# Two moves in the projections of a four-block transformer kernel: rotations split over two chunks, and modulation vectors turned one weight unit later

## The chip, the cores and the metric

The kernel runs on one core of one Trainium2 chip. The metric is the device time of one execution in microseconds, the median over several runs. One profiled execution, taken by the hardware profiler, gives the trace that the rows below come from. In names of the profile PE is TensorE (PEld its weight loads), DVE is VectorE, ACT is ScalarE, POOL is GpSimd, SP is SyncE, which issues the transfers from memory.

## The reference

512 tokens of width 1024 pass through two hybrid layers (`first_block`), then, joined by 256 context tokens, through an even and an odd layer, each with a feed-forward part (`second_block`). All is in float32. What the change touches is the start of a layer: a modulation computed from the conditioning vector, a normed and modulated input, one large in-projection, and rotary embeddings on some of its columns.

```python
def hybrid_layer(x, c_act, positions, w_mod, b_mod, pre_gain, post_gain, w_in, ...):
    mod = c_act @ w_mod + b_mod
    shift, scale, gate = jnp.split(mod[:, None, :], 3, axis=-1)
    h = rms_norm(x, pre_gain) * (1.0 + scale) + shift
    proj = h @ w_in                      # 3088 columns
    (aq, ak, av, ag, rq, rk, rv, rg, gq, gk, gv, gg, ga) = jnp.split(proj, IN_SPLITS, axis=-1)
    aq = apply_rotary(aq.reshape(B, S, ATTN_HEADS, HEAD_DIM), positions, rope_freq)
    ak = apply_rotary(ak.reshape(B, S, ATTN_KV_HEADS, HEAD_DIM), positions, rope_freq)
    a_out = sliding_window_attention(aq, ak, av, sinks) * jax.nn.silu(ag)
    rq = apply_rotary(rq.reshape(B, S, RET_HEADS, RET_DK), positions, ret_freq)
    rk = apply_rotary(rk.reshape(B, S, RET_HEADS, RET_DK), positions, ret_freq)
    ...
    y = jnp.concatenate([a_out, r_out, g_out], axis=-1) @ w_out
    return x + gate * rms_norm(y, post_gain)
```

The even and odd layers of the second block have the same frame with other mixers, and their modulation has two conditions, one for tokens and one for context.

## The kernel before, in words

The program is a list of phases; each engine walks through the list and does its own part of each phase. Most phases end in a barrier of four engines (phase_end); Linear with a residual, the norms and a few others flow into the next.

**Linear** (from line 676) is a projection. Its output columns are cut into chunks, for the sliding layers (layers 0 and 1, `layer_one`, line 1739) five of 512 columns, one of 272 and one of 256; they are counted from 0 here. The rows are token tiles of 128: four in the sliding layers, six (with the context) in the even ones. The 1024 input features of a chunk are read in four weight units (q = 0 to 3) of 256 features.

For each unit SyncE loads the raw weights into one of four slots of `w_raw` (weights_load), ScalarE rounds them to the high half `w_hi` (weights_high, line 288), GpSimd subtracts to get the low half `w_lo` (weights_low, line 295), and TensorE waits for that (weights_use) and does three matmuls for every tile and 128 features (matmul3, lines 306 to 308). w_hi and w_lo have two buffers each: the high half of a unit waits until the unit two before has been used (w_used). Sums stand in banks 0 to 5 of PSUM, one per tile, in rotation over the chunks. VectorE copies them out (line 812; with a residual it multiplies by the gate instead, line 803) and so frees the bank (acc_free). In the unit q = 0 of a chunk the tile with running number i, from 6 on, waits for copy i - 5. With four tiles per chunk the third tile of a chunk is the first that needs a copy of the chunk just before.

**Modulation vectors** are computed beside. A ModJob is half a vector of 512 columns. SyncE loads its matrix in four units, in the same ring of four slots of w_raw between the weight units; a slot is loaded again only when its weight unit has its low half or its mod unit has been summed (ring_slot). VectorE multiplies and adds the units up (sum, line 366) into one of two accumulators and multiplies by a gain (line 377). TensorE adds over the partitions by matmuls with ones into banks 6 and 7 (turn: line 389 for a gate, line 393 for a shift or scale), and ScalarE stores the result (keep, lines 403 and 407). The first sum of a job, into the accumulator of the job two before, waits until that one is turned:

```python
                if q == 0:
                    dve.wait_ge(mod_side[self.k % 2].sem, self.side_bias)
                    if self.k >= 2:
                        dve.wait_ge(mod_turned.sem, turns_before[self.k - 1])
```

Jobs are dealt to chunks. In the sliding in-projections and in the odd in-projection a chunk has one job (chunks 0 to 5, and 0 to 3). In the even in-projection (three chunks of 512, 416 and 256 columns) and in the even out-projection (two chunks of 512) chunks 0 and 1 have two jobs each, with two conditions, so double the sums.

In a chunk the orders are these. VectorE: the sums of the chunk's jobs, the steps "beside" it, the copies of the chunk. ScalarE: the high half of each unit, after each a step "beside" if there is one (silu_columns of a tile, line 1767, which waits for all copies of the chunk before), and after the second unit the keep of the vectors of the chunk before. TensorE: the four units, then the turn of the chunk's jobs.

The steps beside on VectorE in the sliding layers are the rotary embeddings: rotate_columns (line 1754) rotates the four tiles of the attention columns in chunk 2 and of the retention columns in chunk 4; for each tile it calls rotate (line 1215), which is two products into a scratch tile (line 1226), one product (1228) and one sum (1229), all with both inputs in SBUF. In layer 0 chunk 0 also holds the angles.

Of the kernel before, what the change touches and what calls it, by code (L numbers as in the profile page):

```python
# [27 lines left out]
XT = S // P  # L28
# [8 lines left out]
AQ, AK, AV, AG = 0, 512, 640, 768  # L37
RQ, RK, RV, RG = 1280, 1536, 1792, 2048
# [112 lines left out]
def build(nc, a, out):  # L151
    with ExitStack() as ctx:
# [145 lines left out]
        def weights_use(pe, k, n):  # L298

            u = units_done["pe"]  # L300
            units_done["pe"] += 1
            pe.wait_ge(w_lo_ready.sem, u + 1)
            return [w[:, u % 2, 0:k * n].rearrange("p (k n) -> p k n", k=k) for w in (w_hi, w_lo)]
# [12 lines left out]
        class ModJob:  # L316
# [3 lines left out]
            jobs = turns = 0  # L320
# [355 lines left out]
        class Linear:  # L676
# [83 lines left out]
                            steps[q](pool)  # L760

            def tensor(self, pe):
                first = 0
                for (c0, n, tiles), jobs in zip(self.chunks, self.mods):
                    for q in range(4):
                        w = weights_use(pe, 2, n)
                        for i, t in enumerate(tiles, first):
                            if q == 0 and i >= 6:
                                if self.residual:
                                    pe.wait_ge(y_squared.sem, self.residual.y0 + i - 5)  # L770
                                else:
                                    pe.wait_ge(acc_free.sem, self.f0 + i - 5)
                            elif q == 0:
                                wait_bank(pe, self.source, i)
                            for j in range(2):
                                kt = 2 * q + j
                                if first == 0 and i == 0:
                                    wait_features(pe, self.source, kt)
                                ins = matmul3(pe, ps[:, i % 6, 0:n], [HT[:, s, kt, t * P:(t + 1) * P] for s in range(2)],
                                              [w[s][:, j, :] for s in range(2)], start=(kt == 0), stop=(kt == KT - 1))  # L780
                            if q == 3 and t != tiles[-1]:
                                ins.then_inc(acc_ready.sem, 1)
                        ins.then_inc(w_used.sem, 1)
                    if first == 0 and jobs:
                        wait_bank(pe, self.source, 6)
                        wait_bank(pe, self.source, 7)
                    first += len(tiles)
                    for job in jobs:
                        job.turn(pe)

            def vector(self, dve):
                i = 0
# [755 lines left out]
        c1 = np.float32(6.28125)  # L1548
# [190 lines left out]
        def layer_one(l):  # L1739
# [11 lines left out]

            linear = schedule[-1]

            def rotate_columns(which, c0, c1, chunk):
                def step(eng):
                    eng.wait_ge(sines_ready.sem, 3)
                    linear.wait_copied(eng, chunk)
                    for t in range(XT):
                        x = P1[:, t, c0:c1]
                        dve_s.chain(rotate(eng, dve_s, x, x, cos1[:, t, which], sin1[:, t, which], (c1 - c0) // 64, 1, 32, rope_tmp_one))  # L1760
                return step
# [5 lines left out]
                    eng.activation(x, x, ACT.Silu)  # L1767
                return step

            linear.beside["dve"] = {2: [rotate_columns(0, AQ, AV, 1)], 4: [rotate_columns(1, RQ, RV, 3)]}  # L1770
            if l == 0:
                linear.beside["dve"][0] = [first_dve, angles]
            linear.beside["act"] = {c: [silu_columns(c0, n, chunk, t) for t in range(XT)]
# [101 lines left out]
            def act(eng):  # L1875
# [5 lines left out]
                                 dve=lambda eng: eng.tensor_tensor(g_qe[:, :], gqT[:, :], fac2, ALU.mult), clock=1))  # L1881
# [516 lines left out]
        for l in range(DEPTH):  # L2398
            layer_one(l)
# [75 lines left out]
```

## Time and profile before

| | us |
|---|---|
| median of 3 runs | 2690.21 |
| lowest and highest run | 2686.27, 2691.15 |
| profiled execution, its own time | 2677.06 |
| span of its trace | 2675.3 |
| TensorE busy | 2412.1 |
| VectorE busy | 1362.1 |
| GpSimd busy | 1076.0 |
| ScalarE busy | 851.6 |

The span goes from the first to the last instruction of the trace. Busy time counts only instructions that work on data. In a row of the timeline there stand start and duration in us, engine, line of the kernel, operation, output and inputs, partitions and elements, how many were merged, and in brackets how long the engine was idle before and which instruction of which engine ended that.

### The profile page before, as it was taken

How to read it: one execution, taken by the hardware profiler on the slowest of the kernel's cores; microseconds unless marked ns; L12 is line 12 of the kernel's file. 1: busy time of each engine (PE TensorE's matmuls, PEld its weight loads, DVE VectorE, ACT ScalarE, POOL GpSimd, SP SyncE). 2: the span in 40 equal slices, each digit the busy share in tenths (PEclk: the TensorE clock that was granted, in tenths of full speed). 3: DMA queues.
4: the chain of work that ended last, by engine and by line, in shares of the span. 5: the costliest groups of instructions: out<-in, count | busy, mean ns of one | idle time of the engine just before them, and what ended most of it. 6: DMA issues, size and time to landing. Idle time of an engine off the chain costs nothing.

```text
span 2675.3 us, 33460 instructions
## 1 busy us (share of the span) xinstructions
PE 2412.1 (90%) x13114; PEld 1993.8 (75%) x13114; DVE 1362.1 (51%) x2043; ACT 851.6 (32%) x1624; POOL 1076.0 (40%) x793
## 2 busy tenths in 40 slices
PE   3889689988689988888899999999899899999998
PEld 3777467777467865667799998989778667788886
DVE  4885654794654965547753352313479673210112
ACT  2224113214114156563422121211421784322222
POOL 1433326333326233232444242433544343655454
PEclk9999899999899999999999999999999999999999
DMA  7541013440022420002332232324153001222222
GB/s 247 169 146 37 1 56 91 153 155 5 1 64 65 150 56 1 1 9 91 111 103 79 83 107 87 103 67 130 36 185 98 17 1 40 63 98 99 95 95 79
DMA packets 147733, 218.95 MB, mean 82 GB/s; under 512 B 18485, under 2 KB 71125, under 8 KB 147449
## 3 DMA queue, kind: packets, MB, share of 16 engines
q1 hardware_dynamic: 147576, 216.82, 25.2%
q8 instruction: 105, 1.72, 0.3%
q14 instruction: 52, 0.42, 0.0%
HBM read 214.69 MB, written 2.10 MB: 81 GB/s over the span
## 4 chain that ended last, share of the span: by engine, by line
PE 51%; DVE 3%; ACT 2%; POOL 1%; issue 1%; DMA 0%; ACTq 0%; DVEq 0%; POOLq 0%; SPq 0%
PE ps L306 13%; PE ps L307 13%; PE ps L308 13%; PE ps L983 4%; PE ps L1011 3%; PE ps L1033 1%; PE ps L1030 1%; POOL h_transposed L560 1%; PE ps L1272 1%; PE ps L393 1%; DVE x_tokens L842 0%; PE ps L572 0%; DVE mod_acc_aux L366 0%; ACT att_probs_lat L1071 0%; PE ps L1267 0%
## 5 line engine op out<-in xcount | busy, mean ns | idle before, releaser
L295 POOL TENSOR_TENSOR w_lo<-w_raw,w_hi 128x1024 fp32r<-128x1024 f32 (+3 forms) x252 | 590.8, 2346 | 995.7 <-ACT w_hi L288 995.6
L288 ACT ACTIVATE w_hi<-w_raw 128x1024 fp32r<-128x1024 f32 (+3 forms) x252 | 255.7, 1016 | 1167.9 <-PE ps L308 983.8
L306 PE MATMUL ps<-w_hi,h_transposed 128*128 128x512 f32 (+3 forms) x1088 | 418.1, 384 | 57.0 <-POOL w_lo L295 26.5
L307 PE MATMUL ps<-w_lo,h_transposed 128*128 128x512 f32 (+3 forms) x1088 | 409.2, 376 | 0.0
L308 PE MATMUL ps<-w_hi,h_transposed 128*128 128x512 f32 (+3 forms) x1088 | 408.9, 376 | 0.0
L306 PE MATMUL ps<-h_transposed,w_hi 128*128 128x384 f32 (+1 forms) x1056 | 374.7, 355 | 8.1 <-POOL h_transposed L560 6.5
L307 PE MATMUL ps<-h_transposed,w_hi 128*128 128x384 f32 (+1 forms) x1056 | 373.9, 354 | 0.0
L308 PE MATMUL ps<-h_transposed,w_lo 128*128 128x384 f32 (+1 forms) x1056 | 373.9, 354 | 0.0
L366 DVE SCALAR_TENSOR_TENSOR mod_acc_aux<-w_raw,c_act,mod_acc_aux 128x512 f32<-128x512 f32 x280 | 283.4, 1037 | 41.5 <-DMA w_raw<-in_w_mod_dram 19.1
L306 PEld LDWEIGHTS ps<-w_hi,h_transposed 128*128 128x128 f32 x1088 | 213.3, 196 | 103.0 <-POOL w_lo L295 31.1
L1465 DVE TENSOR_TENSOR ffn_full<-ps,ffn_silu 128x768 f32<-128x768 f32 (+1 forms) x44 | 34.2, 819 | 430.8 <-PE ps L308 430.8
L307 PEld LDWEIGHTS ps<-w_lo,h_transposed 128*128 128x128 f32 x1088 | 213.6, 196 | 34.4 <-issue 2.2
L308 PEld LDWEIGHTS ps<-w_hi,h_transposed 128*128 128x128 f32 x1088 | 213.1, 196 | 34.3
L306 PEld LDWEIGHTS ps<-h_transposed,w_hi 128*128 128x128 f32 x1056 | 199.3, 189 | 24.3 <-POOL h_transposed L560 8.7
L308 PEld LDWEIGHTS ps<-h_transposed,w_lo 128*128 128x128 f32 x1056 | 199.5, 189 | 14.0
L307 PEld LDWEIGHTS ps<-h_transposed,w_hi 128*128 128x128 f32 x1056 | 199.5, 189 | 13.9
L306 PE MATMUL ps<-w_hi,ffn_hidden 128*128 128x512 f32 x440 | 174.4, 396 | 0.8 <-POOL ffn_hidden L1394 0.8
L307 PE MATMUL ps<-w_lo,ffn_hidden 128*128 128x512 f32 x440 | 174.5, 397 | 0.0
L308 PE MATMUL ps<-w_hi,ffn_hidden 128*128 128x512 f32 x440 | 172.7, 393 | 0.0
L1108 DVE TENSOR_REDUCE attention_stats<-ps 128x1 f32<-128x768 f32 (+5 forms) x192 | 143.7, 772 | 52.2 <-PE ps L983 44.6
L1479 DVE TENSOR_TENSOR y_tokens<-y_tokens,ps 128x512 f32<-128x512 f32 x60 | 41.2, 686 | 167.0 <-PE ps L308 166.8
L244 PE MATMUL ps<-static_constants 128*128 128x256 f32 x424 | 108.1, 408 | 18.3 <-DVEq L249 8.0
(312 smaller groups left out, 3634.3 us busy)
## 6 DMA issues: line engine op xcount, KB each, us to landing
w_raw<-in_ada_w_dram SPq DMA_DIRECT2D x96, 512.0 KB, 3.8
w_raw<-in_ffn_w_in_dram SPq DMA_DIRECT2D x88, 512.0 KB, 3.5
w_raw<-in_w_mod_dram SPq DMA_DIRECT2D x48, 512.0 KB, 4.5
w_raw<-in_ffn_w_out_dram SPq DMA_DIRECT2D x44, 512.0 KB, 3.5
w_raw<-in_w_in_dram SPq DMA_DIRECT2D x40, 512.0 KB, 4.2
w_raw<-in_w_out_dram SPq DMA_DIRECT2D x16, 512.0 KB, 4.9
w_raw<-in_od_w_in_dram SPq DMA_DIRECT2D x16, 512.0 KB, 3.9
mod_gain<-in_norm_g_dram SPq DMA_DIRECT2D x16, 256.0 KB, 3.9
```

Of the source, the lines that this page charges most:

```text
L244: pe.matmul(ps[:, bank, 0:2 * P], ident, con[:, 0:2 * P], start=True, stop=True)
L288: act.activation(w_hi[:, i % 2, 0:k * n], w_raw[:, u % 4, 0:k * n], ACT.Copy).then_inc(w_hi_ready.sem, 1)
L295: pool.tensor_tensor(w_lo[:, i % 2, 0:k * n], w_raw[:, u % 4, 0:k * n], w_hi[:, i % 2, 0:k * n].bitcast(F32), ALU.subtract).then_inc(w_lo_ ...
L306: pe.matmul(acc, left[0], right[0], start=start, stop=False)
L307: pe.matmul(acc, left[0], right[1], start=False, stop=False)
L308: return pe.matmul(acc, left[1], right[0], start=False, stop=stop)
L366: ins = dve.scalar_tensor_tensor(out=self.acc[:, r], in0=w_raw[:, u % 4, j * HALF:(j + 1) * HALF], scalar=c_act[:, cond, 2 * q + j, c:c + ...
L983: done.append(pe.matmul(sc[:, c:c + m], x["q"][i], x["keys"][i][k][0], start=True, stop=not masks))
L1011: ins = pe.transpose(ps[:, self.turn_bank(r), i * P:(i + 1) * P], self.probs[s % len(self.probs)][:, c:c + P], ident)
L1108: ins = dve.tensor_reduce(dst, src, AX, ALU.max, negate=True)
L1465: dve.tensor_tensor(view(full_t), ps[:, 4 + a * k:4 + (a + 1) * k, 0:w], view(silu_t), ALU.mult)\
L1479: ins = dve.tensor_tensor(y, y, ps[:, t, :], ALU.add)
```

## The change

The first hunk is in Linear.tensor: the turns of a chunk's jobs are no longer issued after its fourth unit but after the first unit of the next chunk; those of the last chunk are issued at the end as before. It holds for every Linear. The second hunk is in layer_one: rotate_columns gets a tuple of tiles, and each of the two rotations is done for tiles 0 and 1 in the chunk of before (2 and 4) and for tiles 2 and 3 in the following one (3 and 5).

```diff
             def tensor(self, pe):
-                first = 0
+                first, before = 0, []
                 for (c0, n, tiles), jobs in zip(self.chunks, self.mods):
                     for q in range(4):
+                        if q == 1:
+                            for job in before:
+                                job.turn(pe)
                         w = weights_use(pe, 2, n)
...
                         wait_bank(pe, self.source, 6)
                         wait_bank(pe, self.source, 7)
                     first += len(tiles)
-                    for job in jobs:
-                        job.turn(pe)
+                    before = jobs
+                for job in before:
+                    job.turn(pe)
...
-            def rotate_columns(which, c0, c1, chunk):
+            def rotate_columns(which, c0, c1, chunk, tiles):
                 def step(eng):
                     eng.wait_ge(sines_ready.sem, 3)
                     linear.wait_copied(eng, chunk)
-                    for t in range(XT):
+                    for t in tiles:
...
-            linear.beside["dve"] = {2: [rotate_columns(0, AQ, AV, 1)], 4: [rotate_columns(1, RQ, RV, 3)]}
+            linear.beside["dve"] = {2: [rotate_columns(0, AQ, AV, 1, (0, 1))], 3: [rotate_columns(0, AQ, AV, 1, (2, 3))],
+                                    4: [rotate_columns(1, RQ, RV, 3, (0, 1))], 5: [rotate_columns(1, RQ, RV, 3, (2, 3))]}
```

## Rows read from the trace of the kernel before

**Rows 1.** The page: busy us of each engine, share of the span, instructions.

```profile
PE 2412.1 (90%) x13114; PEld 1993.8 (75%) x13114; DVE 1362.1 (51%) x2043; ACT 851.6 (32%) x1624; POOL 1076.0 (40%) x793
```

**Rows 2.** Windows of four projections: length, busy us per engine, granted clock, DMA share, GB/s.

```profile
61.00:224.00 163.00, 146.13 (x708) 122.55 (x708) 123.36 (x144) 32.97 (x49) 68.59 (x35) 0.96 0.46 144
446.00:621.00 175.00, 155.25 (x740) 131.38 (x740) 138.63 (x151) 33.95 (x48) 70.62 (x35) 0.91 0.43 138
847.00:952.00 105.00, 90.23 (x475) 79.33 (x476) 89.70 (x127) 20.07 (x50) 40.56 (x41) 0.95 0.33 105
1232.00:1313.00 81.00, 78.04 (x329) 62.49 (x330) 74.00 (x86) 17.42 (x31) 16.11 (x6) 0.94 0.49 159
```

**Rows 3.** TensorE's waits in layer 0, 139 to 225: us, times, longest.

```profile
PE ps L306 <- DVE proj_one L812: 4.9, 2, 3.2
PE ps L306 <- POOL w_lo L295: 4.1, 2, 2.4
```

**Rows 4.** Timeline of layer 0's in-projection, VectorE, and TensorE where chunk 6 begins.

```profile
133.41 0.89 DVE L1226 TENSOR_TENSOR rope_tmp_one<-proj_one,sin_one 128x320 f32<-128x320 f32 x2 [0.21 <-DVE mod_acc_aux L366]
...
136.05 2.96 DVE L1226 TENSOR_TENSOR rope_tmp_one<-proj_one,sin_one 128x320 f32<-128x320 f32 x2
...
146.06 2.48 DVE L812 COPY proj_one<-ps 128x512 f32<-128x512 f32 x4
...
165.65 0.69 DVE L812 COPY proj_one<-ps 128x512 f32<-128x512 f32 x1 [5.90 <-PE ps L308]
...
185.62 0.75 DVE L1226 TENSOR_TENSOR rope_tmp_one<-proj_one,sin_one 128x256 f32<-128x256 f32 x2
...
195.75 2.48 DVE L812 COPY proj_one<-ps 128x512 f32<-128x512 f32 x4
...
211.11 1.47 DVE L812 COPY proj_one<-ps 128x272 f32<-128x272 f32 x4
...
212.16 0.36 PE L306 MATMUL ps<-w_hi,h_transposed 128*128 128x256 f32 x1
```

**Rows 5.** TensorE's waits in layer 1, 515 to 622: us, times, longest.

```profile
PE ps L306 <- DVE proj_one L812: 9.7, 2, 4.9
PE ps L393 <- DVE mod_acc_aux L377: 4.0, 1, 4.0
```

**Rows 6.** Windows in layer 1, columns as in rows 2.

```profile
521.50:604.30 82.80, 66.19 (x321) 56.34 (x319) 80.31 (x92) 14.93 (x24) 27.43 (x13) 0.88 0.40 128
...
602.90:610.50 7.60, 7.59 (x35) 7.59 (x36) 1.35 (x4) 0.18 (x1) 0.00 (x0) 0.50 0.02 5
```

**Rows 7.** Timeline of VectorE, the copies of chunk 5 in layer 1.

```profile
602.78 1.47 DVE L812 COPY proj_one<-ps 128x272 f32<-128x272 f32 x4
```

**Rows 8.** Timelines of the even in-projection, between chunks 0 and 2.

```profile
895.83 2.83 DVE L366 SCALAR_TENSOR_TENSOR mod_acc_aux<-w_raw,c_act,mod_bias 128x512 f32<-128x512 f32 x2
...
896.06 1.96 PE L389 MATMUL ps<-mod_acc_aux,static_constants 128*128 128x512 f32 x4 [1.80 <-ACT gate_rows L403]
...
906.25 0.90 ACT L288 ACTIVATE w_hi<-w_raw 128x832 fp32r<-128x832 f32 x1 [7.60 <-DMA w_raw<-in_ev_w_in_dram]
...
925.01 3.08 DVE L812 COPY proj_even<-ps 128x416 f32<-128x416 f32 x6
```

**Rows 9.** Timelines of the even out-projection, from the end of chunk 0.

```profile
1270.53 3.81 PE L393 MATMUL ps<-static_constants,mod_acc_aux 128*128 128x1 f32 x32
...
1274.33 1.40 DVE L366 SCALAR_TENSOR_TENSOR mod_acc_aux<-w_raw,c_act,mod_bias 128x512 f32<-128x512 f32 x2
...
1286.20 1.06 ACT L288 ACTIVATE w_hi<-w_raw 128x1024 fp32r<-128x1024 f32 x1 [9.09 <-DMA w_raw<-in_ev_w_out_dram]
...
1308.35 3.75 PE L389 MATMUL ps<-mod_acc_aux,static_constants 128*128 128x512 f32 x8
```

**Rows 10.** Lines of VectorE by form, layer 1, 521 to 604: busy us, mean ns.

```profile
L366 DVE SCALAR_TENSOR_TENSOR mod_acc_aux<-w_raw,c_act,mod_acc_aux 128x512 f32<-128x512 f32 x42 | 47.8, 1178 | 1.5 <-DMA w_raw<-in_ada_w_dram 0.8
...
L366 DVE SCALAR_TENSOR_TENSOR mod_acc_aux<-w_raw,c_act,mod_bias 128x512 f32<-128x512 f32 x6 | 4.2, 746 | 0.1
```

## The prediction, made before the change was run

> **What bounds the kernel now.** I read the page first. TensorE is busy 90% of the span [rows 1], so a change that removes no matmul can only win or lose its idle time and its time at the lower clock. The windows view of the four projections in which something happens [rows 2] shows where that is: the sliding in-projections of layers 0 and 1 hold 163 and 175 us with 146 and 155 us of TensorE work, the even in-projection 105 with 90, the even out-projection 81 with 78. VectorE is busy for 123 to 139 us of the sliding stretches and for 74 of the 81 us of the even out-projection.
>
> Layer 0's waits [rows 3] name two reasons: 4.9 us for VectorE's copies and 4.1 us for the low half of a weight unit. The timeline of VectorE [rows 4] explains both. The rotation of chunk 1 runs from 133.4 to 146.1, the copies of chunk 2 only then. Tile 2 of chunk 3 needs the bank of the first of them, so TensorE stops after 12 matmuls; ScalarE sits in silu_columns until the last copy and makes the next high half after it. From 195.75 the same happens at chunk 5. But between sums and copies of chunk 3 VectorE idles 5.9 us: there is room for half a rotation. Layer 1 has the same waits for copies, longer (9.7 us), plus 4.0 us in which the turn of the last vector waits for its sum [rows 5]. Its windows row from the first rotation that would be moved to the copies of chunk 5 says that VectorE works 80.3 of 82.8 us [rows 6]: there is no room there.
>
> **Part 1, the halved rotations.** The instructions stay the same. In layer 0 two rotations took 7.3 us where one of them met a w_lo on GpSimd (2.96 us for a pair of products instead of 0.89) and the other two 5.3 [rows 4]. Chunk 2 keeps the first two, so its copies start at 140.8 instead of 146.1; TensorE does not stop, and the low half behind the silu is ready at about 147.5 instead of 153.1, against an end of chunk 3's first unit at 145.2 plus a turn. Gain there 5.5 us. The other two (5.3 us) fall into the 5.9 us of idle and cost nothing; were that cover gone, chunk 3's copies would be late by what is missing. In chunk 4 half of the rotation of 185.6 to 195.75 goes (about 5.1 us); chunk 5 starts 5.4 us earlier and has neither the 1.7 nor the 2.4 us stall, so its second unit starts near 191 and it ends near 200.5 rather than 211.3. Now VectorE is late next: copies of chunk 4 end at 188.7 (before 198.2), the sums of chunk 5 take 13.0 us as from 198.2 to 211.1 [rows 4], to 201.7, then the moved half, 5.1, to 206.8. First copy 207.2. Tile 2 of chunk 6 waits for it, a stall of some 4.6 us. Of chunk 6 (11.8 us for 96 matmuls, from 212.2 [rows 4] to the end of the stretch in rows 2) 84 matmuls are left, 10.3 us, plus one turn, 0.9, plus the lower clock. For that: after the 4.05 us wait of layer 1 the granted clock was 0.50, the level of 1.2 GHz, for 7.6 us [rows 6]; half of this, 3.8, is the upper bound, 0 the lower; the gap here is about as long, but the shorter slow stretches elsewhere in this trace make me take 2.5. End 220.9 against 223.9: **layer 0 gains 3.0 us** (bounds 1.7 and 5.5).
>
> Layer 1: VectorE leaves chunk 2 earlier by two rotations, 5.3 us, and gets all of it back in chunks 3 to 5, where it is saturated. Its last copies start near 603.3 instead of 602.8 [rows 7]. TensorE gains 5.5 us at chunk 3 and spends it in front of chunks 4, 5 and 6. What stays: half of chunk 6's first unit, 12 matmuls, is done before, 1.5 us, minus 0.5 for the later copy, minus rounding. **Gain 0.6 us** (bounds a loss of 1.5, a gain of 2.5).
>
> **Part 2, the turns moved.** No matmul is added. In the sliding layers and the odd in-projection each chunk has one vector. Its sum needs the turn of the vector two before (ModJob.sum, first unit), which is still an entire chunk old; so VectorE waits for nothing new. Where the turn hid in a stall it now stands in the path: 0.45 us once in layer 0, inside the sum above. On ScalarE keep stands in front of the high half of the third unit and now waits for a turn that comes after the first unit. Counted from the end of that unit: turn and wait 1.2, keep 0.6, high 1.1, low 2.4 to 2.9 (ScalarE's and GpSimd's timelines; a high half is in rows 9) gives 5.3 to 5.8 us, and TensorE needs it after a turn of 0.5 and a unit of 5.45, at 5.9. I cost it at nothing; the cover is 0.1 to 0.6 us per chunk. Odd in-projection: its units are longer or its halves smaller; nothing.
>
> The two **even projections** are different: two vectors per chunk, and the first sum of chunk 1 needs the turn of the first vector of chunk 0. Today that turn comes in front of chunk 1. Afterwards it comes behind its first unit. Queued behind that wait on VectorE are all sums of chunk 1 and its copies; and behind the sums, since SyncE refills a slot of the ring only when it is summed, the third and fourth weight unit.
> Even in-projection [rows 8]: the sums start at 895.8; now chunk 1's first unit starts at 893, takes 6.9, the gate turn 1.9: 901.9. One collision at 895.8 (2.83 us for two sums instead of 1.4) goes, so VectorE is 4.7 us late. The 1.80 us of TensorE in front of 896.06 go too. The third unit's high half started 10.4 us after the sums; now 9.0 after 901.9, low half done at 913.9, TensorE wants it at 910.9: stall 3.1. VectorE copies chunk 1 from 929.6 instead of 925.0, TensorE follows to 934.4 and then turns 3.6 us, so ScalarE's keep, its high half and latent_squares come 3.5 us later, and they carry the end (meansq, rstd, norm, last copies). **Loss 3.5 us** (bounds 1.5 and 5.1, the latter TensorE's own delay).
> Even out-projection [rows 9]: the turn (3.8 us) ran while the gated copies and squares freed the banks. Now TensorE starts chunk 1 with the first square, 1272.2; a unit is 8.5 us; 1280.7. First turn done 1282.6 where the sums began at 1274.3: VectorE 8.3 late. The third unit's high half began 11.9 us after the sums; taking off half of a collision, at 1293.8, low half done 4.0 later, 1297.8. TensorE is through two units and the turn at 1293.0: stall 4.8. Two units more and 2.0 us of lower clock: 1316.8 instead of 1308.4. VectorE ends at 1314 and is no longer what is waited for. **Loss 8.4 us** (bounds 5.0, without slow clock and with an early load, and 10.5).
>
> Sum: 3.5 + 8.4 - 3.0 - 0.6 = **+8.3 us**; I round it down to +7.5, because in the even stages every later start also spares collisions. The profiled execution took 2677.1 us, so 2684.6; the median of the three runs is 2690.2, 13 us above it, so 2697.7 in that measure.
>
> **A rule against the change.** Rows 4 show a rotation's products at 2.96 us instead of 0.89 beside a w_lo. The Trainium skill (SBUF — State Buffer, Who interferes with whom) says that a VectorE instruction with two SBUF inputs and a GpSimd instruction that reads SBUF exclude each other for the whole instruction, whoever started first. By it the moved rotations, with both inputs in SBUF, could also hold up w_lo in chunks 3 and 5, and a w_lo that is late by one rotation product uses up the cover of 0.1 to 0.6 us. The copies read PSUM and never lengthen (2.48 us for four each time), which agrees.
>
> **Rivals.** An effect of 0.2%, 5.4 us, is about the least that a measurement of this kernel tells from none; so slower is above 2695.6, faster below 2684.8.
> - *Cancelling* (0.29): the same mechanism, with the stalls at full clock: layer 0 gains 5.5, layer 1 1.5, the even losses are 2.5 and 5. About +0.5, 2690.7. For it: the clock bounds; against it: all four must go the kind way.
> - *Worse* (0.08): ScalarE's keep delays the third unit wherever a vector is turned. 15 moved turns in the sliding and odd projections at 0.4 us is 6 us: 2704. It decides once turn, keep, high and low last over 5.9 us.
> - *Faster* (0.13): VectorE's chain of the sliding layers gets shorter because the shifted sums meet fewer w_lo. In layer 1 a sum lasts 1178 ns on average against 746 of the six that met none [rows 10]: 42 times 0.43 is 18 us of collisions. Each avoided is up to 2.1 us. It decides from 7 avoided in both layers (13.7 us): then 2683 or less; I take 2682. Against it: the number of w_lo in the stretch stays.
> - That the edit does not do what it says I exclude: both hunks act on instruction order alone.
> The forecast has 0.50, own range 2694 to 2702, a fifth of it under 2695.6. Slower 0.40 + 0.08, same 0.29 + 0.10, faster 0.13. Range 2685 to 2704: below lies the faster case, above the tail of the worse one.
>
> **What would show it.** In the profile after: no wait for proj_one copies before chunk 3 and 5 in layer 0, a new one of 4 to 5 us in chunk 6; in layer 1 waits for copies in chunks 4, 5 and 6 (about 8 us) and the last copies near 603; in both even projections VectorE idle 6 and 8 us in front of the first L366 of chunk 1, released by TensorE, and a w_lo wait of 3 and 5 us. Wrong would be: VectorE not waiting there, or chunk 6 of layer 0 running through.

## The result, and the profile after the change

The changed kernel takes **2695.76 us** (median of 22 executions, 2686.53 to 2706.35), the kernel before 2688.7 us (22 executions, 2680.52 to 2693.7). The ratio is 1.0025, with a 95% interval of 1.0014 to 1.0035: slower by 7.1 us. I had predicted 2697.7 us and +7.5 us.

The profiled executions differ by much more: 2706.35 us (span 2704.6) after, against 2677.06 before. The first is the slowest of its 22, the second lies 12 us under its median. So I use the profiles for what happens where, and the timed ratios (the median time of a kernel over that of the kernel before, run beside it) for what it costs. The page after, to be held against [rows 1], has 22 us more of TensorE at the same number of matmuls, which is lower clock and not work:

```profile
span 2704.6 us, 33468 instructions
...
PE 2434.6 (90%) x13114; PEld 2008.5 (74%) x13114; DVE 1361.1 (50%) x2043; ACT 852.4 (32%) x1624; POOL 1079.2 (40%) x793
```

The same four projections as in [rows 2], in the windows view of the changed kernel (length, busy us per engine, granted clock, DMA share, GB/s), here from first to last matmul, turns included:

```profile
59.94:224.12 164.18, 150.07 (x708) 126.33 (x708) 126.17 (x142) 32.95 (x48) 68.91 (x34) 0.92 0.46 143
453.60:629.47 175.87, 155.28 (x740) 131.30 (x740) 137.80 (x149) 33.10 (x46) 71.33 (x34) 0.92 0.44 137
858.66:964.60 105.94, 90.50 (x472) 78.47 (x472) 85.55 (x116) 20.22 (x50) 39.20 (x40) 0.95 0.33 104
1250.86:1336.60 85.74, 80.04 (x328) 63.26 (x328) 71.74 (x85) 16.46 (x29) 15.72 (x6) 0.92 0.51 151
```

From first to last matmul the kernel before needed 162.7, 173.9, 100.5 and 79.8 us. In this pair of profiles layer 0 and layer 1 are 1.5 and 2.0 us longer, the even in-projection 5.4, the even out-projection 5.9. Further profiles below show how much of each repeats.

**Layer 0.** TensorE's waits after 139 us, to be held against [rows 3]:

```profile
PE ps L306 <- DVE proj_one L816: 4.7, 1, 4.7
PE ps L306 <- POOL w_lo L295: 2.1, 2, 1.2
```

The two waits for copies in front of chunks 3 and 5 have become one in chunk 6, as forecast (4.6 us). The timeline of VectorE shows the path to it, and the last two lines, of TensorE, the stall and the turn that now stands in chunk 6 (start, length, operation, tiles, and in brackets the idle time ahead of it with what ended that):

```profile
131.83 2.79 DVE L1230 TENSOR_TENSOR rope_tmp_one<-proj_one,sin_one 128x320 f32<-128x320 f32 x2 [0.21 <-DVE mod_acc_aux L366]
...
136.37 3.09 DVE L1230 TENSOR_TENSOR rope_tmp_one<-proj_one,sin_one 128x320 f32<-128x320 f32 x2
...
141.22 2.48 DVE L816 COPY proj_one<-ps 128x512 f32<-128x512 f32 x4
...
156.92 2.94 DVE L1233 TENSOR_TENSOR proj_one<-proj_one,rope_tmp_one 128x640 f32<-128x640 f32 x1
...
187.99 2.48 DVE L816 COPY proj_one<-ps 128x512 f32<-128x512 f32 x4
...
209.07 1.48 DVE L816 COPY proj_one<-ps 128x272 f32<-128x272 f32 x4
...
209.56 0.58 PE L306 MATMUL ps<-w_hi,h_transposed 128*128 128x256 f32 x1 [4.69 <-DVE proj_one L816]
212.29 1.70 PE L393 MATMUL ps<-static_constants,mod_acc_aux 128*128 128x1 f32 x8
```

Compare with [rows 4], and count from the first matmul, 61.2 before and 59.9 after. The copies of chunk 2 start 81.3 us in, against 84.9 before and 79.6 in the forecast: both halves of the rotation left in chunk 2 met a w_lo (2.79 and 3.09 us, where an undisturbed pair of products takes 0.89), and I had counted one. The moved half in chunk 3 lasts from 155.13 to 162.51, 7.4 us and not 5.3, because one sum (L1233, 0.82 us when undisturbed) took 2.94 beside the w_lo that GpSimd ran from 156.78:

```profile
156.78 2.40 POOL L295 TENSOR_TENSOR w_lo<-w_raw,w_hi 128x1024 fp32r<-128x1024 f32 x1 [5.86 <-ACT w_hi L288]
```

The Trainium skill (SBUF — State Buffer, Who interferes with whom) says that two such instructions exclude each other. The trace agrees, and shows that VectorE is the one held up in these three cases, by 1.9 to 2.2 us: this w_lo kept the 2.40 us that it has alone, the two beside the products of chunk 2 took 2.78 and 2.59. So a collision here costs the rotation some 2.1 us and the low half 0.4 us at most.

**Layer 1.** TensorE's waits from 515 to 632, against [rows 5], then the stall in chunk 6 and the turn behind it, then three windows around it, columns as above:

```profile
PE ps L306 <- DVE proj_one L816: 13.1, 4, 7.3
PE ps L306 <- POOL w_lo L295: 3.9, 3, 1.4
```

```profile
612.56 0.58 PE L306 MATMUL ps<-w_hi,h_transposed 128*128 128x256 f32 x1 [7.34 <-DVE proj_one L816]
615.28 3.41 PE L393 MATMUL ps<-static_constants,mod_acc_aux 128*128 128x1 f32 x16
```

```profile
605.20:612.50 7.30, 0.02 (x1) 0.00 (x0) 7.06 (x12) 0.00 (x0) 1.39 (x1) 0.80 0.14 36
612.50:621.50 9.00, 8.94 (x42) 8.94 (x43) 1.05 (x4) 0.70 (x2) 1.27 (x1) 0.50 0.01 2
621.50:629.50 8.00, 7.97 (x60) 7.77 (x59) 1.27 (x3) 0.63 (x1) 1.29 (x1) 0.89 0.00 0
```

The wait of the turn for its sum is gone, and the wait for copies has grown from 9.7 to 13.1 us. The granted clock fell during the 7.3 us in which TensorE did nothing (mean 0.80), and was 0.50, the level of 1.2 GHz, for the 9 us behind them.

**The even projections.** VectorE's waits in the in-projection (899 to 966) and in the out-projection (1286 to 1337), one line from each answer, and what TensorE waits for later, in the order of time:

```profile
DVE mod_acc_aux L366 <- issue: 6.0, 1, 6.0
...
DVE mod_acc_aux L366 <- issue: 8.1, 1, 8.1
```

```profile
911.34 3.75 PE L389 MATMUL ps<-mod_acc_aux,static_constants 128*128 128x512 f32 x8
925.35 0.46 PE L306 MATMUL ps<-w_hi,h_transposed 128*128 128x416 f32 x1 [3.44 <-POOL w_lo L295]
933.12 0.46 PE L306 MATMUL ps<-w_hi,h_transposed 128*128 128x416 f32 x1 [0.69 <-POOL w_lo L295]
942.03 0.36 PE L306 MATMUL ps<-w_hi,h_transposed 128*128 128x256 f32 x1 [1.88 <-DVE proj_even L816]
...
1299.06 3.71 PE L393 MATMUL ps<-static_constants,mod_acc_aux 128*128 128x1 f32 x32
1314.81 0.50 PE L306 MATMUL ps<-w_hi,h_transposed 128*128 128x512 f32 x1 [2.23 <-POOL w_lo L295]
```

The profile gives no releaser for the 6.0 and 8.1 us ("issue"), where TensorE had been forecast as the releaser, but the sums start at 913.31 and 1300.99, in the middle of the turns at 911.34 and 1299.06: when the first vector's half of the turn is done. Experiment 7 tests that link. I had forecast 6 and 8 us. Of the stalls that follow, the 3.44 us had been forecast at 3.1, the 0.69 and 1.88 not by name; the out-projection's 2.23 was to be 4.8.

### The profile page after: what moved, and what is told of

It is laid out like the page before. It is cut to its first block, busy times and chain, and to the rows that moved or that the text cites. A ratio compares the mean times of both kernels' runs of the same rounds, so it can differ in the third digit from the quotient of the medians.

```text
span 2704.6 us, 33468 instructions
## 1 busy us (share of the span) xinstructions
PE 2434.6 (90%) x13114; PEld 2008.5 (74%) x13114; DVE 1361.1 (50%) x2043; ACT 852.4 (32%) x1624; POOL 1079.2 (40%) x793
## 4 chain that ended last, share of the span: by engine, by line
PE 48%; DVE 5%; issue 2%; ACT 2%; POOL 1%; DMA 1%; ACTq 0%; DVEq 0%; POOLq 0%; SPq 0%
PE ps L306 13%; PE ps L307 13%; PE ps L308 12%; PE ps L987 4%; PE ps L1015 2%; PE ps L1037 1%; DVE mod_acc_aux L366 1%; PE ps L1034 1%; PE ps L1276 1%; POOL h_transposed L560 1%; DVE x_tokens L846 0%; PE ps L572 0%; PE ps L393 0%; PE ps L1271 0%; ACT att_probs_lat L1075 0%
## 5 line engine op out<-in xcount | busy, mean ns | idle before, releaser
L366 DVE SCALAR_TENSOR_TENSOR mod_acc_aux<-w_raw,c_act,mod_acc_aux 128x512 f32<-128x512 f32 x280 | 272.0, 996 | 45.7 <-DMA w_raw<-in_ada_w_dram 20.5
L244 PE MATMUL ps<-static_constants 128*128 128x256 f32 x424 | 116.6, 432 | 17.0 <-DVEq L249 8.0
```

Source lines behind the costliest of these rows:

```text
L244: pe.matmul(ps[:, bank, 0:2 * P], ident, con[:, 0:2 * P], start=True, stop=True)
L366: ins = dve.scalar_tensor_tensor(out=self.acc[:, r], in0=w_raw[:, u % 4, j * HALF:(j + 1) * HALF], scalar=c_act[:, cond, 2 * q + j, c:c + ...
```

## The experiments

In the profiled runs, projections are measured from first to last matmul, and each run has one profile. "The sliding layers" are layers 0 and 1. Theory at the outset: the even projections lose by VectorE's wait for the first vector's turn, the sliding ones gain a little. Rivals: ScalarE's keep behind the late turn delays the third unit; or the cost lies in the halved rotations.

**1 and 2. Both kernels once more**, without an edit, since the profiles differ by more than the medians.

> The changed kernel once more, beside the parts of it, for a second profile. Expected 7 us over the kernel before (ratio 1.0025). In its profile the even in-projection should again be about 5 us longer and the even out-projection about 6 us longer than before, VectorE idle about 6.0 and 8.1 us before the first sum of their chunk 1; if these stretches differ by more than 1 us from the first profile of the changed kernel, the clock moves them and not the waits.

> The kernel before once more, for a second profile. Its first one was 13 us under the median of its runs. Between layer 0's in- and out-projection it lasted 164.3 us there at a mean clock of 0.94, in both profiles of the changed kernel 171 us at 0.88. If that difference belongs to the change, this profile shows 164 us again; if it is the state of the clock in one execution, it shows 168 to 172 us and the span is near 2687.

Measured: after 2694.89 us, ratio 1.0025 (1.0011 to 1.0040), span 2699.7; before 2685.47 us, span 2683.7. Projections of layer 0, layer 1, even in, even out: 163.3, 175.9, 105.5, 84.1 after and 164.0, 175.6, 100.7, 79.8 before. So the even losses repeat (4.8 and 4.3 us), and the sliding layers differ by under a microsecond. The out-projection is 1.6 us shorter than in the first profile of the same kernel, more than the 1 us that I had named as the sign that the clock has a part. It has: 64 to 80 us into that stretch the granted clock is 0.89 in the first profile and 1.00 in the second, and VectorE's wait (8.1 us) and the w_lo stall behind it (2.2 us) are the same in both. What also repeats in direction is a stretch that the change does not touch, from layer 0's in-projection to its out-projection:

```profile
223.90:388.20 164.30, 128.84 (x727) 92.39 (x726) 102.34 (x206) 45.44 (x130) 54.28 (x76) 0.94 0.04 14
```

```profile
224.10:391.60 167.50, 132.75 (x727) 94.52 (x726) 102.45 (x206) 45.45 (x130) 54.32 (x76) 0.91 0.04 14
```

```profile
224.10:395.30 171.20, 136.92 (x727) 98.48 (x726) 102.42 (x206) 45.55 (x130) 54.47 (x76) 0.88 0.04 13
```

These are the windows of the kernel before, of the same again, and of the changed kernel (171.3 us, 0.88, in its second profile). The same 727 matmul records take 128.8, 132.8 and 136.9 us; the granted clock is 0.94, 0.91 and 0.88, and the length follows it. The 167.5 us fall between the 164 that would have put the difference down to the change and the 168 to 172 that would have put it down to the single execution, so this run leaves it open; experiment 7 has more to say.

**3. The halved rotations alone.** No turn is moved.

```diff
-            linear.beside["dve"] = {2: [rotate_columns(0, AQ, AV, 1)], 4: [rotate_columns(1, RQ, RV, 3)]}
+            linear.beside["dve"] = {2: [rotate_columns(0, AQ, AV, 1, (0, 1))], 3: [rotate_columns(0, AQ, AV, 1, (2, 3))],
+                                    4: [rotate_columns(1, RQ, RV, 3, (0, 1))], 5: [rotate_columns(1, RQ, RV, 3, (2, 3))]}
```

> Only the rotations are split, the turns stay before the next chunk. Theory (late turns cost, split rotations gain in layer 0 alone): layer 0's in-projection 2 to 5 us shorter than before, layer 1's within 2 us, even and odd ones unchanged; in all 2 to 6 us faster than before. Rival (the rotations themselves cost, because they meet more w_lo and hold up chunks 5 and 6): same or slower than before by up to 4 us.

Measured: 2680.76 us, ratio 0.9975 (0.9965 to 0.9986). Layer 0's projection 158.9 us, layer 1's 168.7, the even ones as before (100.6, 79.8). This half of the change is a gain of 6.7 us (3.8 to 9.4). I had expected layer 1 within 2 us of before; it came out 5 to 7 us shorter.

**4. The moved turns alone.** The rotations stay whole in chunks 2 and 4; the turns are moved as in the change (its first hunk alone).

> Only the turns are moved, rotations as before. Theory: the even in-projection 4 to 5 us longer, the even out-projection 6 to 8 us longer, sliding ones within 1 us (a turn that hid in the stall at chunk 3 or 5 still fits); in all 10 to 12 us slower than before. Rival (keep in front of the third high half delays weights wherever a vector is turned): the sliding layers lose too, 3 us or more each, in all 16 us or more.

Measured: 2692.01 us, ratio 1.0010 (1.0000 to 1.0019). Layer 0 164.4, layer 1 169.1, even 105.8 and 84.1. So layer 1 is 5 us or more shorter with the late turns as well, and the even projections lose alike. That gain, and an out-projection that lost 4.3 us and not 6 to 8, are why the total is some 3 us slower and not the 10 to 12 that I had expected. The two halves, 0.9975 and 1.0010, would make 0.9985; together they make 1.0025.

**5. The change, but chunks with two vectors turn as before.**

```diff
-                    before = jobs
+                    now = jobs if len(jobs) == 2 else []
+                    for job in now:
+                        job.turn(pe)
+                    before = [] if now else jobs
```

> As the changed kernel, but chunks with two vectors (the even in- and out-projection) turn them at the end of their own chunk as before. Theory: the 10 to 12 us of the even projections are gone, so 2 to 5 us faster than the kernel before, and the even stretches as long as before. Rival (sliding layers carry the loss): still slower than before by 3 us or more.

Measured: 2682.26 us, ratio 0.9984 (0.9970 to 0.9997). Layer 0 161.7, layer 1 175.8, even 100.8 and 79.8: the four together 518.1 us, against 516.9 and 520.1 in the two profiles of the kernel before, so the gain in time does not show in these stretches. Taking the late turns out of the even projections turns +7.1 us into -4.3.

**6. Late turns only where there are two vectors.** The rotations as before, and `len(jobs) == 1` in place of `len(jobs) == 2` in the edit of experiment 5.

> Turns moved only in the chunks with two vectors, rotations as before. Theory (the first sum waits for the late turn): even in-projection 5 us longer, even out-projection 4 to 6 us longer, VectorE idle 6 and 8 us there; sliding and odd stretches as in the kernel before; 10 to 11 us slower in all. Rival (the sum of parts is not the whole, the even losses are given back in the stages behind): under 5 us slower.

Measured: 2695.49 us, ratio 1.0039 (1.0025 to 1.0053). Even 105.8 and 84.2, layer 1 175.4; layer 0, whose program is that of the kernel before, 166.4. The loss of the even projections by itself is 10.5 us (6.7 to 14.2) by time, 9.5 us by the two stretches. A little of it is given back right behind: from the first matmul of the out-projection to the first of the odd in-projection it is 704.2 us here (704.3 in experiment 4, 703.8 in experiment 1, 707.1 in the first profile of the changed kernel), and 700.3 to 700.8 in every profile in which the first turn comes at once, so 3.0 to 4.0 us are left in the first three.

**7. The change, but the first of two vectors is turned at once**, the second behind the next chunk's first unit.

```diff
-                    before = jobs
+                    now = jobs[:1] if len(jobs) == 2 else []
+                    for job in now:
+                        job.turn(pe)
+                    before = jobs[len(now):]
```

> The changed kernel, but where a chunk has two vectors the first of them is turned at the end of its chunk as before and only the second behind the next chunk's first unit. The sum that waits needs only the first. Theory: VectorE's idle 6 and 8 us in front of the sums go, and with them the waits for w_lo; even in-projection 99 to 101 us, even out-projection 79 to 81, 9 to 11 us faster than the changed kernel. Rival (ScalarE's keep of a late turn in front of the third high half is what costs): both stay more than 3 us longer than before, at 104 and 83.

Measured: 2684.63 us, ratio 0.9999 (0.9984 to 1.0013). Layers 163.9 and 176.2, even in-projection 100.0, out-projection 78.3 us. VectorE's timeline of the in-projection, and TensorE's turns beside it:

```profile
899.56 3.67 DVE L819 COPY proj_even<-ps 128x512 f32<-128x512 f32 x6
903.15 2.77 DVE L366 SCALAR_TENSOR_TENSOR mod_acc_aux<-w_raw,c_act,mod_bias 128x512 f32<-128x512 f32 x2
...
900.06 1.88 PE L389 MATMUL ps<-mod_acc_aux,static_constants 128*128 128x512 f32 x4
908.59 1.88 PE L389 MATMUL ps<-mod_acc_aux,static_constants 128*128 128x512 f32 x4
```

The sums follow the copies without idle time, although a turn of the second vector (908.59) still comes late and ScalarE's keep with it. Neither even stretch is longer than before the change. This is the experiment that tells the wait from the keep: the wait of VectorE for the **first** vector's turn makes the loss, and the keep of a late second turn does not. By time it is 7 us faster than the changed kernel, less than the 9 to 11 expected. From layer 0's in- to its out-projection, where its program is that of the changed kernel, it took 167.4 us at 0.91, not 171.2 at 0.88.

**8. The fourth corner of the square: the late turns of chunks with one vector alone.** The rotations as before, the edit of experiment 5.

> The rotations as before; of the turns only those of chunks with one vector behind the next chunk's first unit, so that the even projections are as before. The fourth corner of a square: before, a_rot_only and a_single_only (0.9984) are the other three. Theory (both edits gain the same idle time of TensorE in the sliding projections, and together they give part of it back; the loss in the even projections of 10 us adds to either): 1.0010 of a_turns_only less 0.0039 of b_even_only, so 0.997, layer 1's projection about 169 us, even in-projection 100.5 and out-projection 79.8. Rival (the effects only add, and the difference between the runs is chance): ratio 0.9975 of a_rot_only against 0.9984 of a_single_only makes the late single turns alone 1.0009, layer 1 at 174 us or more.

Measured: 2681.88 us, ratio 0.9985 (0.9974 to 0.9996); layer 0 163.2, layer 1 168.8, even 101.0 and 79.8. Its interval holds neither the 0.997 of the theory nor the 1.0009 of the rival, and it is a little closer to the first. The square is now: neither 1, halved rotations 0.9975, late single turns 0.9985, both 0.9984. If they added, both would be 0.9960. The gap of 0.0024 is hardly more than what the three intervals leave open together, so the times alone make it likely, no more. Layer 1 in the profiles is plainer: 173.9, 175.6, 175.4 with neither; 168.7 with halved rotations; 168.8 and 169.1 with late turns; 175.9, 175.9, 175.8 and 176.2 (experiments 1, 5 and 7) with both. Each edit alone saves 5 to 7 us there, and the second takes it back. Layer 0 has no such order: 162.7, 164.0 and 166.4 with neither, 158.9 with halved rotations, 163.2 and 164.4 with late turns, 161.7 to 164.2 with both.

The four kernels' windows, up to the copies of chunk 5 and from there to the end of the projection, show in which part. Before:

```profile
446.50:602.78 156.28, 137.74 (x628) 114.07 (x628) 135.00 (x143) 32.00 (x43) 67.54 (x32) 0.93 0.48 153
602.78:620.40 17.62, 17.49 (x112) 17.30 (x112) 2.74 (x8) 1.44 (x3) 2.58 (x2) 0.75 0.01 3
```

Halved rotations alone:

```profile
447.70:604.19 156.49, 139.57 (x653) 116.25 (x654) 133.80 (x143) 31.95 (x44) 67.91 (x32) 0.95 0.49 154
604.19:616.50 12.31, 12.26 (x89) 12.06 (x88) 2.77 (x8) 1.26 (x2) 2.58 (x2) 0.86 0.00 1
```

Late single turns alone, with two windows ahead of the copies too:

```profile
452.40:608.60 156.20, 139.92 (x639) 117.57 (x640) 131.07 (x142) 31.83 (x43) 67.03 (x32) 0.92 0.49 152
608.60:621.20 12.60, 12.49 (x104) 12.09 (x102) 2.76 (x8) 1.33 (x3) 3.81 (x3) 1.00 0.07 21
...
589.50:594.00 4.50, 4.41 (x20) 4.41 (x21) 4.43 (x8) 1.28 (x3) 1.59 (x1) 0.50 0.02 4
594.00:599.00 5.00, 5.00 (x23) 5.00 (x24) 4.93 (x6) 1.03 (x3) 1.72 (x2) 0.50 0.47 135
```

Both:

```profile
453.60:612.07 158.47, 138.37 (x640) 114.59 (x640) 135.05 (x143) 31.77 (x43) 68.76 (x32) 0.95 0.49 152
612.07:629.50 17.43, 16.91 (x100) 16.71 (x100) 2.75 (x7) 1.33 (x3) 2.56 (x2) 0.68 0.00 1
```

Up to the copies VectorE sets the pace, at 156.2 to 156.5 us in three of these profiles, whatever the edit, and 158.5 with both; but the two other profiles of layer 1 with neither edit have 158.0 and 157.9, so these 2 us belong to the execution as much as to the edits. The tail is 17.6, 12.3, 12.6 and 17.4 us, and it repeats: 17.5 and 17.6 with neither, 12.6 with late turns in experiment 4, 17.4 to 17.6 with both. It depends on how much TensorE had got done and on its clock. With late turns alone the last stall (5.98 us) comes in front of 589.6, and the clock is at half while VectorE would have held TensorE up anyway; the tail runs at 1.00. With halved rotations a wait of 4.05 us ends at 599.84 and the low level ends near 607.6. With both, the early stalls are small (1.1 to 3.2 us), all that is saved is collected in the last one, 7.34 us, and the 9 us at half clock fall on the tail, where only TensorE works. That is what the rows show in order; that the place of the stall is what decides was not tried by itself.

**9. The attention rotation split, both halves of the retention rotation moved to chunk 6**, behind the copies of chunk 5, the last that TensorE waits for in the projection. Turns as before.

```diff
-            linear.beside["dve"] = {2: [rotate_columns(0, AQ, AV, 1)], 4: [rotate_columns(1, RQ, RV, 3)]}
+            linear.beside["dve"] = {2: [rotate_columns(0, AQ, AV, 1, (0, 1))], 3: [rotate_columns(0, AQ, AV, 1, (2, 3))],
+                                    6: [rotate_columns(1, RQ, RV, 3, (0, 1, 2, 3))]}
```

> Turns as in the kernel before; attention rotation split over chunks 2 and 3, the retention rotation (9 to 10 us) moved whole to chunk 6, where VectorE has no sums and idles 9.2 us in layer 0 and 14 us in layer 1. Theory (VectorE's late copies are what stops TensorE in front of chunks 5 and 6): waits for copies in chunks 5 and 6 go, layer 0's in-projection 154 to 157 us (before 162.7), layer 1's 162 to 166 (before 173.9), in all 12 to 18 us faster than before. Rival (the late rotation delays the copies of chunk 6 and so the end): no faster than the kernel with split rotations and turns as before, 0.9975.

Measured: 2669.82 us, ratio 0.9944 (0.9924 to 0.9963). Layer 0 154.1, layer 1 165.2; the copies of chunk 5 start 141.3 and 148.5 us in, against 149.9 and 156.2 before. In chunk 6 VectorE had idled for 9.2 and 14.1 us in front of that chunk's own copies. The rotation now stands in front of them, and they hardly notice: the last one starts 0.5 us after the last matmul in layer 0, at once in layer 1.

**10 and 11. The parts of it**: the attention rotation alone split (retention whole in chunk 4), and the retention rotation alone put into chunk 6 (attention whole in chunk 2).

> Before, with the attention rotation alone split over chunks 2 and 3, the retention rotation whole in chunk 4, the turns as before. Theory (the gain of the split lies in the attention half, whose second half falls into VectorE's idle time behind chunk 3's sums in layer 0): layer 0's projection about 159 us as with both rotations split, copies of chunk 5 at about 148, ratio 0.997. Rival (the retention split carries it, as chunk 4 no longer holds chunk 5's sums up): layer 0's projection stays at 162 to 164, ratio 0.999 to 1.001.

> Before, with the attention rotation whole in chunk 2 and the retention rotation whole in chunk 6, the turns as before. Theory (what gains is that the retention rotation leaves VectorE's chain in front of the copies of chunk 5, and lies in chunk 6 where VectorE idles): layer 0 and 1 projections 156 to 159 and 166 to 168 us, ratio 0.995 to 0.996, between the halved rotations (0.9975) and both changes (0.9944). Rival (the split of the attention rotation is the larger part): ratio 0.998 or more. In either case the copies of chunk 5 start 4 to 6 us earlier than before in both layers.

Measured: 2684.18 us, ratio 0.9980 (0.9967 to 0.9994), layers 157.7 and 175.2; and 2678.62 us, ratio 0.9968 (0.9954 to 0.9982), layers 156.3 and 165.4. These two do add: 0.9948 against the 0.9944 of experiment 9. Splitting the attention rotation helps layer 0 (5 to 6 us), which has the idle time, and does nothing in layer 1, which has none; taking the retention rotation off the chain helps both. In layer 0 the copies of chunk 5 start 144.9 and 143.5 us in. Halving the retention rotation alone, to which the 168.7 us of experiment 3 in layer 1 would then belong, was not run. The ratio of the second is a little above what I gave for it, 0.995 to 0.996, though its stretches came out at the short end of what was said, or below.

**12. All that helped together**: the rotations of experiment 9, and of two vectors the second late; chunks with one vector turn as before. The edit of the turns, against the changed kernel's place for them (its `if q == 1` stays):

```diff
-                    before = jobs
+                    for job in jobs[:1]:
+                        job.turn(pe)
+                    before = jobs[1:]
                 for job in before:
                     job.turn(pe)
```

> Attention rotation split over chunks 2 and 3, retention rotation whole in chunk 6, and of a chunk's vectors the first turned at once and only the second behind the next chunk's first unit (so chunks with one vector turn as before). Theory (the loss in the even projections comes from the wait for the first vector's turn alone, and the second turn does no harm late): projections of layers 0 and 1 as in b_both_late (154 and 165 us), even in- and out-projection 100.0 and 78.3 us as in b_first_at_once, against 100.7 and 79.8; ratio 0.9936, 0.001 under b_both_late. Rival (the late second turn gives nothing once TensorE's clock differs): 0.9944 or more.

Measured: **2665.48 us, ratio 0.9924 (0.9906 to 0.9942)**, faster than both kernels. TensorE's waits in layer 0 (100 to 213) and layer 1 (500 to 600), one answer under the other:

```profile
PE ps L306 <- POOL w_lo L295: 1.3, 2, 0.7
PE ps L393 <- DVE mod_acc_aux L377: 0.5, 1, 0.5
...
PE ps L393 <- DVE mod_acc_aux L377: 4.1, 2, 3.4
PE ps L306 <- POOL w_lo L295: 2.9, 1, 2.9
PE ps L306 <- DVE proj_one L818: 1.4, 1, 1.4
```

Waits for copies, 13.1 us in layer 1 after the change, are 1.4 here. The stretches are 152.0, 163.3, 99.2 and 78.2 us. Against experiment 9 the intervals overlap, so what the late second turn adds is not shown by time. By profile the out-projection repeats its 78.3 of experiment 7, 1.5 us less than before, but only some 0.3 us of that is left at the start of the odd in-projection; the in-projection's 99.2 and 100.0 lie within what kernels with its program unchanged have (99.1 to 101.0).

## Why the prediction was right

**The sum.** Predicted +8.3 us before rounding, +7.5 after; measured +7.1 (3.8 to 9.4). Its two groups can be timed apart. The sliding layers: forecast 3.0 and 0.6 us of gain, experiment 5 gives 4.3 (0.8 to 8.1). The even projections: forecast 3.5 and 8.4, 11.9 us of loss, experiment 6 gives 10.5 (6.7 to 14.2). Inside the groups four terms were mis-sized, and they cancel; that the total came within half a microsecond of the rounded forecast is luck. The stretches say it plainly. The sliding layers, forecast at 3.6 us of gain, gave none: over the profiles with one program in both layers the means are 163.3 and 175.9 us with the change (four profiles) and 164.4 and 175.0 with neither edit (three), 1.1 us gained and 1.0 lost. Where the 4.3 us of experiment 5 come from is therefore open. The even projections, forecast at 11.9 us of loss, cost 5.1 us in the in-projection and 4.3 in the out-projection, of which 3.0 to 4.0 are left at the start of the odd in-projection. What is right in the forecast is its mechanism for the even projections, the wait of the first sum for the late turn, and the sign.

**Layer 0, 3.0 us of gain.** It was about 1 us: 164.2, 163.3, 161.7 and 163.9 us with the change, 162.7, 164.0 and 166.4 with neither edit. Two steps failed. The copies of chunk 5 start 149.1 us in (146.9 to 149.1 in the four profiles), where the forecast had 146.0: 1.7 us of it stand already at chunk 2's copies (the second collision), 3.0 at the end of chunk 4's. And from that copy to the end it took 15.05 us (14.8 in the others), not 13.7, since the granted clock was 0.74 there:

```profile
209.50:224.10 14.60, 14.54 (x92) 14.36 (x92) 2.33 (x7) 1.33 (x3) 2.57 (x2) 0.74 0.01 2
```

3.0 less 3.1 less 1.4 is the 1.5 us of loss of that profile. With the rotations halved and no turn moved (experiment 3) the copies start 146.6 us in and the stretch takes 158.9: without the late turns the step's gain is there, in that one profile.

**Layer 1, 0.6 us of gain.** It lost about 1 (175.8 to 176.2 against 173.9, 175.6 and 175.4), inside the bound of 1.5 I had given. That VectorE is saturated and gives nothing back was right. What failed is to have costed the two edits each on the kernel before, as if the tail were the same: either alone gains 5 to 7 us.

**Even in-projection, 3.5 us of loss.** It was 5.1 (105.9, 105.5 with the change, 105.8 in experiments 4 and 6, against 100.5 to 100.8). The wait (6.0), the first w_lo stall (3.4) and the copies of chunk 1, 82.6 us in instead of 77.4, came as said; the step that failed was that the end would follow less late than these. It was the upper bound, TensorE's own delay, that held.

**Even out-projection, 8.4 us of loss.** It was 5.9 in the first profile and 4.3 to 4.4 in the three others (experiments 1, 4 and 6), under the lower bound of 5.0. The wait was right (8.1). The w_lo stall behind it was 2.2 and not 4.8: low half ready 13.8 us after the start of the sums and not 15.2, since the load came sooner, and TensorE's unit and turn ended 11.6 us after it and not 10.4, at a granted clock of 0.84: this fall of the clock came ahead of the stall and was paid out of it. And the 2.0 us set down for a lower clock behind the stall did not come in the three other profiles (1.00 from there to the end of the chunk); in the first it cost 1.6.

```profile
1302.60:1312.60 10.00, 9.97 (x37) 7.80 (x37) 9.75 (x15) 1.24 (x2) 0.61 (x1) 0.84 0.66 202
```

**ScalarE's keep at nothing** held: behind the late single turns of the changed kernel the w_lo waits are 1.2 us at most from chunk 3 of layer 0 on and 1.4 in layer 1, and experiment 8, with all of these turns late, is not slower but faster than before. The odd in-projection, also put at nothing, took 142.6 and 142.5 us in the two profiles of the changed kernel against 141.2, but 141.3 to 141.4 with the same late turns in experiments 4, 5, 7 and 8; what makes that 1.3 us is open. The *worse* rival is out. *Cancelling*, at 1.0002, lies outside the interval: it asked for 7 us of gain in the sliding layers, where 4.3 were measured, and 7.5 of even loss, where it was 10.5; each of these alone would still lie in its interval. *Faster* by fewer collisions: the mean of the 42 sums in layer 0 fell from 1344 to 1243 ns, 4.2 us, but the eight products (four pairs) into the scratch tile of the attention rotation went from 5.6 to 7.7 us, its four sums from 3.3 to 5.4, and VectorE's busy time in the stretch rose from 123.4 [rows 2] to 126.2 us.

```profile
L366 DVE SCALAR_TENSOR_TENSOR mod_acc_aux<-w_raw,c_act,mod_acc_aux 128x512 f32<-128x512 f32 x42 | 52.2, 1243 | 13.6 <-DMA w_raw<-in_w_mod_dram 12.5
```

## What to carry to other kernels

When a producer's turn is put off behind other work, ask first who waits for the buffer that it frees: with two buffers and two jobs per stage, the first job of the next stage waits for the first turn of this one, and a helper engine with everything queued behind it stands still. Split the pair, and put off only the job whose buffer nobody needs yet.

Work on an engine that sets the pace stays in the way when it is halved; it is out of the way behind the last copies that another engine waits for. With halved rotations the copies of chunk 5 in layer 1 start 156.5 us in, no earlier than the 156.2 before; with the retention rotation moved to chunk 6 they start 147.9 us in (experiment 11). By time the move was worth 8.6 us (4.8 to 12.4) and the halving 6.7 (3.8 to 9.4), so the times alone don't rank the two; move and split together (experiment 9) were worth 15 us.

Two edits that win the same idle time have to be tried in all four combinations; here each gained in layer 1, and both together gained nothing.

## What was not expected of the hardware

Stretches of the program that no edit touches came out up to 7 us apart, by the granted clock alone: from layer 0's in- to its out-projection 164.3 (0.94) and 167.5 us (0.91) before, 171.2 and 171.3 (0.88) after, and 165.0 to 171.2 among the other kernels. Nor does it go by the program of layer 0: with that of the changed kernel it was 171.2 and 171.3 us, 171.2 again in experiment 5, and 167.4 in experiment 7. So the same code costs more or less from one execution to the next, and whether what ran just ahead has a part in it the one profile per kernel cannot tell. Executions of the changed kernel spread over 20 us, those of the kernel before over 13. Why is open; no run here was made for it, and how much of the +7.1 us is of this kind is not known.

What a stall of TensorE costs beyond its own length depends on what comes next. After 7.3 us of it the granted clock was 0.50 for 9 us of pure TensorE work; after 6.0 us (experiment 8) it was 0.50 for 9.5 us and more, beside a VectorE that was the slower of the two anyway, and the tail of the projection was 5 us shorter.
